# A three-block transformer kernel: an earlier start, a split normalisation, reordered routing, a re-cut fill, and matmuls of constants in five waits

## The reference, cut to what matters

```python
# block 1: differential attention;  block 2: pooling mixer;  block 3: forgetting attention + RG-LRU
h = layer_norm(ALPHA * h + mixer(h), g, b)          # blocks 1 and 2 (block 3: rmsnorm, residual x + mixer)
logits = h @ w_router + b_router                    # 4 group logits, 32 expert logits
g = argmax(group logits); e1, e2 = top2(expert logits of group g)
y[token] = sum_k gate_k * (silu(h @ w_gate[e_k]) * (h @ w_up[e_k])) @ w_down[e_k]
h = layer_norm(ALPHA * h + y, g, b)
# differential attention, per head of 8:
o = (softmax(q1 k1') - lam * softmax(q2 k2')) @ v
o = o * rsqrt(mean(o*o) + 1e-5) * sub_g * (1 - lambda_init)   # then @ w_o
# block 3's attention, per head of 8: softmax(q k' / 8 + decay) @ v, a width of 64
```

## Time and profile before

| | |
|---|---|
| median of 3 runs | 2135.12 us (2132.74 to 2141.25) |
| the profiled execution's own time | 2146.18 us |
| its span, first to last instruction | 2144.1 us |
| mean granted TensorE clock | 0.973 |
| busy: PE, DVE, ACT, POOL | 2006.3, 694.8, 404.4, 117.2 us |

### The profile page before, as it was taken

How to read it: one execution, slowest core, us unless ns; L and a number is a source line. 1 busy time by engine, 2 the same in 40 slices (tenths; PEclk the granted TensorE clock), 3 DMA queues, 4 the chain that set the end, 5 groups by cost and what they waited for, 6 DMA issues and landing times.

```text
span 2144.1 us, 25582 instructions
## 1 busy us (share of the span) xinstructions
PE 2006.3 (94%) x10125; PEld 1074.9 (50%) x10125; DVE 694.8 (32%) x1668; ACT 404.4 (19%) x873; POOL 117.2 (5%) x140
## 2 busy tenths in 40 slices
PE   8999989999999999799999999999699989899787
PEld 4444445545545454645655455454544445665454
DVE  0155546321111111635421111111747223532114
ACT  1033432111111111111111111111233222112112
POOL 0000001100000000000100000000100001111100
PEclk9999998999999999999999999999899999999999
DMA  9611102799999999922799999999921111699995
GB/s 331 176 59 40 40 20 101 275 419 420 420 421 420 421 420 391 334 99 70 285 419 419 421 421 421 421 420 400 330 85 39 39 40 43 208 355 420 419 419 211
DMA packets 123826, 595.59 MB, mean 278 GB/s; under 512 B 15751, under 2 KB 43287, under 8 KB 60767
## 3 DMA queue, kind: packets, MB, share of 16 engines
q1 hardware_dynamic: 110559, 568.06, 66.7%
q0 software_dynamic: 13184, 26.40, 3.7%
HBM read 572.95 MB, written 37.01 MB: 284 GB/s over the span
## 4 chain that ended last, share of the span: by engine, by line
PE 79%; DMA 12%; DVE 5%; ACT 2%; issue 2%; another core or an unknown queue 0%; SPq 0%; DVEq 0%; ACTq 0%
PE bank L979 21%; PE bank L1022 10%; PE bank L653 10%; PE bank L895 10%; DMA ring<-in_moe_w_up_dram 6%; DMA ring<-in_w_up_dram 5%; PE bank L795 5%; PE bank L665 4%; PE bank L639 3%; PE bank L1153 1%; PE bank L749 1%; PE bank L722 1%; PE bank L886 1%; PE bank L1114 1%; PE bank L709 1%
## 5 line engine op out<-in xcount | busy, mean ns | idle before, releaser
L979 PE MATMUL bank<-ring,work 128*64 128x512 f32 (+1 forms) x3008 | 559.5, 523 | 29.2 <-DMA ring<-in_w_up_dram 25.9
L979 PEld LDWEIGHTS bank<-ring,work 128*64 128x64 f32 x3008 | 222.9, 137 | 361.9 <-issue 336.2
L1022 PE MATMUL bank<-ring,work 128*64 128x512 f32 x1280 | 295.8, 600 | 3.9 <-DVE work L1839 3.9
L1839 DVE COPY work<-bank 128x256 f32<-128x256 f32 (+1 forms) x96 | 36.5, 380 | 691.7 <-PE bank L887 691.7
L895 PE MATMUL bank<-work 128*128 128x128 f32 x2112 | 253.3, 278 | 0.0
L895 PEld LDWEIGHTS bank<-work 128*128 128x128 f32 x2112 | 240.8, 192 | 6.3 <-issue 2.0
L653 PE MATMUL bank<-hT,ring 128*128 128x512 f32 x512 | 237.7, 607 | 0.7 <-ACT work L1216 0.7
L1307 ACT ACTIVATE work<-bank 64x512 f32<-64x512 f32 x96 | 56.6, 589 | 547.2 <-PE bank L1022 541.9
L1022 PEld LDWEIGHTS bank<-ring,work 128*64 128x64 f32 x1280 | 84.3, 136 | 143.9 <-issue 129.0
L653 PEld LDWEIGHTS bank<-hT,ring 128*128 128x128 f32 x512 | 94.2, 194 | 109.7 <-issue 107.9
L1295 ACT ACTIVATE work<-bank 64x512 f32<-64x512 f32 (+1 forms) x96 | 49.7, 518 | 475.1 <-PE bank L979 475.1
(11 more groups left out here) (306 smaller groups left out, 1691.8 us busy)
## 6 DMA issues: line engine op xcount, KB each, us to landing
ring<-in_moe_w_down_dram SPq DMA_DIRECT2D x128, 1024.0 KB, 16.7
ring<-in_moe_w_gate_dram SPq DMA_DIRECT2D x126, 1024.0 KB, 15.5
ring<-in_moe_w_up_dram SPq DMA_DIRECT2D x126, 1024.0 KB, 17.3
ring<-in_w_down_dram SPq DMA_DIRECT2D x32, 1024.0 KB, 25.4
ring<-in_w_gate_dram SPq DMA_DIRECT2D x31, 1024.0 KB, 22.9
ring<-in_w_up_dram SPq DMA_DIRECT2D x31, 1024.0 KB, 23.6
ring<-in_attn_w_qkv_dram SPq DMA_DIRECT2D x12, 1024.0 KB, 13.6
work<-y_rows SPq DMA_DIRECT2D x12, 1024.0 KB, 6.9
```

The lines of the kernel that those rows point to most:

```text
L979: mm = pe.matmul(GU2[s % 2][BLK * a:BLK * a + BLK, 0:F], xgT[pair % 2][:, per * kk + k, BLK * of_pair:BLK * of_pair + BLK], v[a][:, k, :], ...
L1022: mm = pe.matmul(DN[BLK * n:BLK * n + BLK, :], hT_[:, 2 * kk + k, :], v[:, k, 512 * n:512 * n + 512], start=(kk + k == 0), stop=(2 * kk + ...
```

## The change

- Start: SP issues unit 0 after the second tile of `x`, units 1 and 2 after the fourth, and the rope table after them. PE turns two tiles, then runs the first unit's matmuls tile by tile (`turn_beside`), turning tiles 2 and 3 between them. POOL's broadcasts wait for the last tile of `x`.
- First attention's end: root and scaling for tiles 0 and 1 are moved ahead (DVE step 39, ACT step 40, before its last `copy_turned`); those for tiles 2 and 3 stay behind the last step. PE turns tiles 0 and 1, begins `head(0)`, and turns tile 2 after `project(0, 0)` and tile 3 after `project(0, 1)`.
- Heads, all three: PE's second half of `project(3, 1)` is moved before `ranks(1)`. DVE's `choose(1)` and `place(0)` are moved before `part(3, 0)`, `place(1)` stays after it; the three memsets go from tile 0 to tile 1.
- `keep_busy(n)` is new: n matmuls of constants, 512 columns each, into bank 0, whose result nobody reads. n = 13 after `sum_last_pair` at the end of mixtures 0 and 1, behind a wait for the gathered rows of tile 0; n = 4 in each head between `gather(2)` and `ranks(3)`.
- `fill`: the same 16 matmuls a head pair are cut otherwise over the steps, and the empty eighth step is dropped, so that pair 2 begins at g = 7 and pair 3 at g = 15.

```diff
             for i in range(T):
                 sp.dma_start(h[:, i, :], t["x"][0, P * i:P * i + P, :]).then_inc(x_loaded[i], 16)
+                if i == 1:
+                    load(0)
+            load(1)
+            load(2)
             sp.dma_start(work[:, 16384:17408], t["rope"]).then_inc(par.rope, 16)
-            for u in range(first["wo"]):
+            for u in range(3, first["wo"]):
                 load(u)
...
+            def keep_busy(n):
+                for _ in range(n):
+                    pe.matmul(bank[0][:, :], ident, con[:, 0:512], start=True, stop=True)
...
                 sum_last_pair(l, 0)
                 sum_last_pair(l, 1)
+                pe.wait_ge(routing.gathered[0], 16 * (l + 1))
+                keep_busy(13)
                 for tt in range(T):
...
                     for tt in range(T):
+                        if ready and kk == 0:
+                            ready(tt)
                         for k in range(4):
...
-            turn("x", h)
-            pe.wait_ge(tiles_copied, turns["x"].copied_all)
-            for n in range(2):
-                project_b(first["v"] + 2 * n, hT, bank[4 * n:4 * n + 4])
+            def turn_beside(tt):
+                if 1 <= tt < T - 1:
+                    turn("x", h, K, range(tt + 1, tt + 2))
+                pe.wait_ge(tiles_copied, 2 * tt + 2)
+
+            turn("x", h, K, range(2))
+            project_b(first["v"], hT, bank[0:4], turn_beside)
+            project_b(first["v"] + 2, hT, bank[4:8])
...
-            turn("o1", o1[:, :, 4 * P:8 * P], 4)
+            def turn_o1(tt):
+                turn("o1", o1[:, :, 4 * P:8 * P], 4, range(tt, tt + 1))
+
+            turn_o1(0)
+            turn_o1(1)
...
                 project(0, 0)
+                if l == 0:
+                    turn_o1(2)
                 project(0, 1)
+                if l == 0:
+                    turn_o1(3)
                 project(1, 0)
...
                 turn_one(2)
+                project(3, 1, range(4, K))
                 ranks(1)
-                project(3, 1, range(4, K))
                 router(2)
...
                 gather(2)
+                keep_busy(4)
                 ranks(3)
...
             for c in range(1, 4):
-                for x, sizes in enumerate((((1, 2), (1, 2), (1, 1)), ((1, 2), (1, 2), (1, 0), (1, 0)))):
+                queries = ((1, 2), (1, 2), (1, 1)) if c == 1 else ((0, 2), (1, 1), (1, 1), (1, 1))
+                for x, sizes in enumerate((queries, ((1, 1), (1, 2), (1, 1), (1, 0)))):
...
-                fill.append([])
...
             for step in range(5 * 8 + 1):
+                if step == 40:
+                    act.wait_ge(at.var, 2)
+                    act.activation(orstd[:, 0:2, 4:8], orstd[:, 0:2, 4:8], ACT.Sqrt).then_inc(at.std, 1)
                 if step > 8:
                     copy_turned(step - 9)
...
+                if step == 39:
+                    dve.wait_ge(at.o, 30)
+                    dve.tensor_scalar(orstd[:, 0:2, 4:8], sumsq[:, 0:2, 4:8], 1.0 / P, 1e-5, ALU.mult, ALU.add)\
+                        .then_inc(at.var, 1)
...
+            for t0 in (0, 2):
+                if t0:
+                    dve.wait_ge(at.o, 32)
...
+                dve.wait_ge(at.std, 2 + t0 // 2)
+                link(dve.reciprocal(orstd[:, t0:t0 + 2, 4:8], orstd[:, t0:t0 + 2, 4:8]))
+                for tt in range(t0, t0 + 2):
+                    for hh in range(4, 8):
+                        ins = normal_head(tt, hh)
+                    ins.then_inc(tiles_written, 1)
...
                 for tt in range(T):
+                    if tt == T - 1:
+                        choose(1)
+                        place(0)
                     part(tt, 0)
...
                     if tt == T - 1:
-                        choose(1)
-                        place(0)
                         place(1)
                     part(tt, 1)
...
+            pool.wait_ge(x_loaded[T - 1], 16)
             bcast(subg, t["attn_sub_g"], par.sublam, 128)
```

More of the change, by code:

```diff
@@ L656, in project_t, with project_b @@
                         mm.then_inc(units_used if half else half_unit, 1)
-            def project_b(u, operand, banks):
+            def project_b(u, operand, banks, ready=None):
                 for kk in range(2):
@@ L1260, in _ @@
                         .then_inc(at.raw, 1)
-            act.wait_ge(at.var, 2)
-            act.activation(orstd[:, :, 4:8], orstd[:, :, 4:8], ACT.Sqrt).then_inc(at.std, 1)
+            act.wait_ge(at.var, 3)
+            act.activation(orstd[:, 2:4, 4:8], orstd[:, 2:4, 4:8], ACT.Sqrt).then_inc(at.std, 1)
             turned("o1", 4)
@@ L1583, in _ @@
             dve.wait_ge(at.added, 8)
[L1584 to L1591, removed]
+            for t0 in (0, 2):
+                if t0:
+                    dve.wait_ge(at.o, 32)
+                    dve.tensor_scalar(orstd[:, 2:4, 4:8], sumsq[:, 2:4, 4:8], 1.0 / P, 1e-5, ALU.mult, ALU.add)\
+                        .then_inc(at.var, 1)
+                dve.wait_ge(at.std, 2 + t0 // 2)
[4 more added lines that the diff above has]
+                    ins.then_inc(tiles_written, 1)
             link(dve.tensor_scalar(slots1, con[:, C_SLOT:C_SLOT + BLK], 1.0, None, ALU.add))
@@ L1689, in mixture @@
                 for tt in range(T):
+                    if tt == T - 1:
+                        choose(1)
+                        place(0)
                     part(tt, 0)
-                    if tt == 0:
+                    if tt == 1:
                         dve.memset(gpad, -BIG)
```

## The result

The changed kernel took 2120.09 us (2118.37 to 2122.30, four runs) against 2135.18 (2132.74 to 2141.25, four runs): a ratio of 0.9919, interval 0.9896 to 0.9942. It is 15 us faster; 31.5 were forecast, and the time lies at the upper edge of the whole range given (2092 to 2120), outside the 2095 to 2112 in which the forecast itself was put. The profiled execution after took 2122.30, with a span of 2120.5: between the two profiled spans 23.6 us are gone, between the medians 15. Both differences need explaining.

What follows compares the result with a forecast made beforehand. PE was taken as the bound (busy 2006 of 2144.1 us), with its idle time and lower-clock work to be won. Eight terms summed to -31.5 us, from 2135.1 to 2103.6; forecast range 2095 to 2112, whole range 2092 to 2120.

Steps and rivals of the forecast that it cites:

- Start, -5.5: Kernel start: values begin 6.9 us earlier, added tile blocks cost 2.1, clock returns 0.7; -5.5 us, between -3 and -7.
- First attention's end, -4.0: End of first attention: `project(0, 0)` 6.0 us earlier, less turned tiles and lower clock; -4.0, between -2.3 and -6.
- head(0), -8.0: Before mixture 0: filled waits, earlier `choose` and constants remove a lower-clock stretch; -8.0 us, between -5 and -11.3.
- head(1), +0.5: Before mixture 1: constants delay `ranks(3)` by 2.4 us, partly given back by quicker gathers; +0.5, between -1.5 and +3.
- head(2), -3.4: Before mixture 2: earlier `ranks(2)`, quicker `gather(3)` and less waiting, against constants costing 2.2; -3.4 us, between 0 and -5.
- Mixture 0's end, 0.0: After mixture 0: 13 constants delay the first turn by 2.5 us; turn and projection give it back; 0.0, -1.8 to +2.5.
- Mixture 1's end, -1.3: After mixture 1: constants fit the wait; turn and projection give 0.9 + 1.5, DVE takes back 1.1; -1.3, 0 to -2.
- Second attention, -9.8: Re-cut fill: 3.7 us less waiting, and lower-clock losses in pairs 1 and 2 won; -9.8, between -3.7 and -10.5.
- rival of constants at the lower clock: Blocks of 13 and heads' fours: constants don't hold the clock, each costs 1.72 us; total 2145 us, chance 0.04.
- Theory 1: Set before follow-ups: terms right in kind; the profiled execution before had a low stretch in head(0) that other executions lack.
- Theory 2: Set before follow-ups, for the missing gain: the matmuls of constants cost what the orders win.
- Theory 3: Set before follow-ups, for the missing gain: what is won early is lost in the weight stream.

Runs made afterwards that it cites:

- end_only: The kernel before with the new end of the first attention alone (and the heads' three memsets behind tile 1): 2130.27 us, ratio 0.9983.
- b_again: The kernel before, unchanged, run and profiled a second time: 2135.36 us, ratio 0.9995 to the kernel before.
- fill_only: The kernel before with the re-cut fill of the second attention alone: 2124.66 us, ratio 0.9940.
- best: The changed kernel without the blocks of 13 constants and with the four constants in head(0) alone: 2106.34 us, ratio 0.9867 to the kernel before.
- after: The changed kernel with all its edits, in its first measurement and profile: 2120.09 us, ratio 0.9919 to the kernel before.
- start_only: The kernel before with the new start alone (SP's order, PE's `turn_beside`, POOL's wait): 2138.36 us, ratio 0.9998.
- no_constants: The changed kernel without any matmuls of constants (both blocks of 13, all three of four): 2114.26 us, ratio 0.9904 to the kernel before.
- a_again: The changed kernel, unchanged, run and profiled a second time: 2116.24 us, ratio 0.9906 to the kernel before.

## Where the prediction was right and where its sum went too far, point by point

- **Start, -5.5.** The values come 6.5 us earlier. The first q and k projection comes at 73.2 to 76.2, mean 74.6, in the five traces with the old start and at 67.5 to 71.2, mean 69.2, in the nine with the new one: -5.4. Right for the place. By itself it moved no median; six of its twelve runs lie where head(0)'s bad outcome was traced.
- **First attention's end, -4.0.** It is 5.2 to 6.1 shorter, less the 1.05 of turned tiles that went into head(0): 4.1 to 5.0, and 4.1 by `end_only`. Load and root took 1.49 and left 0.96 of the cover, as the rows said and not as the Trainium skill has it (ScalarE: Activation LUTs, What ACT_TABLE_LOAD costs), whose 1.38 of drain would have used it up: no drain is to be seen between the load's end at 306.45 and the root at 306.47.
- **head(0), -8.0: the step that failed**, together with the sentence "A difference carries over". Profile to profile it measured -9.2. Against the ordinary execution, `b_again`, it is +0.5 to -0.1: 59.0 before, 59.5 and 58.9 after, with the 1.05 of turned tiles counted above in it, so that the term itself is -0.5 to -1.2. It is made of the order, about +1 (60.1 and 60.3 without tiles and constants), and the four constants, about -2 (61.0 and 61.1 without, 58.6 to 59.5 with them). The prediction had noted that the profiled execution lay 11 us above the median, and didn't ask which of its terms was made of those 11. The low stretch at 0.50 and the wait of 4.55, whose cause it had not found in the trace, were just that. A part of the low clock it named did stay: the first gather still takes 3.78.
- **head(1), +0.5.** It measured +2.3 between the profiles, +2.2 to 2.9 against `b_again`, inside the bound of 3. How much of it the fours are isn't settled: without them it took 83.5 to 87.0 in five traces with the new order, with them 85.3 to 86.6 in four.
- **head(2), -3.4.** It measured -3.0. The parts were other than forecast in size: the order gives 6 (60 to 54.0) where only 1.0 to 1.2 of issue wait stands before the last gather, and the fours take back 2.8.
- **Mixture 0's end, 0.0.** It measured +1.8 and -1.6, as worked out; against `b_again` +1.8 and -0.9.
- **Mixture 1's end, -1.3, the other step that failed.** It measured +3.7: 2.4 up to the sums, most of it the wait on issue, 1.7 for the sums at the lower clock, and the turn gave 0.65 for 0.9. The first projection gave nothing: after 3.52 us idle it was at the lower clock as before. The prediction had no term for a wait that 21 more matmuls ahead bring with them.
- **Second attention, -9.8.** It measured -8.6 between the profiles, -9.9 to -12.4 against `b_again`; -11 to -13 by `fill_only`. Eight steps took 29.6 where 29.5 was forecast for a pair, but only in the middle; the first eight took 33.0.
- **A part that no edit touches:** the eight matmuls of eight rows took 11.58 after and 8.65 in `best`, as the clock fell in them early or late. That is 2.8 of the profiled pair's difference; the interval is 12.3 to 12.6 in four traces, with the change's parts and without them (`after`, `fill_only`, `start_only`, `end_only`), and 9.4 to 10.2 in the other ten.
- **Sums in it that are off.** The good ends of the terms add up to 45.1, so 2090 and not 2092. In the rival of constants at the lower clock the fours delay `ranks(3)` by 5.7 only in heads 1 and 2; against head(0)'s wait of 3.93 it is 3.0, so 14.5 in all and not 17. Neither changes the forecast.

From -31.5 to the -23.6 of the profiled pair: mixture 1's end 5.0, the eight-row matmuls 2.8, head(1) 1.8, and the others -1.7 together. From -23.6 to the -15 of the medians: before's profiled execution lay 11.0 above its median, after's 2.2. On the second chip the medians differ by 19.7. Counted against an ordinary execution, head(0) misses some 7, mixture 1's end 5.0 and head(1) 1.8; with these the forecast would have been about -18, between the two differences measured. That the time still fell into the range given owes something to the range: its upper end was there for other cases, some edits that miss and clock stretches that only move.

Theory 1 holds for the larger part. Theory 2 holds for the fours in head(2) (2.8) and for mixture 1's end (over 3), about 6 us in all; the gains in head(0) (2) and in the projections after mixture 0 (1.5, against a delay of 1.8) give back about 2 of it. That `no_constants` is no faster for all that has to do with its waits on issue, 1.34 in head(0) and 2.48 in head(2), where `best` has none and 0.97. `best`, without the 13s and those fours, lies 0.4% (8 us) under `a_again` by the ratios. Theory 3 falls: mixtures 0 and 1 take 470 to 475 us and mixture 2 278, however early they start. The rival of constants at the lower clock falls with 0.86 us each.

## What to carry to other kernels

Before a term of a sum is read from a profile, set that execution's own time against the median: if it lies above by more than most runs scatter, some stretch in it may be bad luck, and a second profiled execution of the same kernel says which. Here an order that takes waits away (the fill, 11 us) was worth far more than filler that occupies them. The filler paid 2 us in head(0), where work at the lower clock stood behind it, about nothing after mixture 0, and cost 2.8 in head(2), where only 0.96 was idle. A wait longer than the filler was no guarantee either: after mixture 1, 3.52 us stayed idle behind it and the projection was at the lower clock as before. A gain that doesn't show in the median may be there in half the executions; look at the single times before calling it nothing.

## What the runs showed of the hardware that was not expected

- The same idle time of 2.36 us before `ranks(1)` was followed by 17 us at the lower level (1.2 GHz, a granted 0.50 and 0.51) in two traces; in three others the same 17 us had 0.90, 0.90 and 0.80, the rest being at 2.4 GHz (`b_again`, `fill_only`, `end_only`). What decides isn't visible here. Both long executions also have DVE's wait of 4.55 before its last logits, and in `b_again` and `fill_only` it is 0.60 and 0.61.
- The clock also fell where PE had no wait at all: in the eight matmuls of eight rows PE was busy throughout, and the granted clock went from 0.92 to 0.50, in `after` for their last 8.6 us, in `best` for their last 2.7.
- A wait of PE on issue came and went with what stands ahead in its program: 3.2 to 3.4 before mixture 1's last sums in all three kernels with 21 more matmuls ahead, none on issue there in the other eleven traces. Before the last gathers of head(1) and head(2) no such rule shows: the profile puts waits of 0.97 to 2.67 on issue in some traces and of 0.74 to 3.65 on DVE in others, in head(1) even for one and the same program (2.08 on DVE in before, 1.41 on issue in `b_again`). The instructions come in packets of about 16 KB (0.92 MB in 56, the page's q8 row). That these waits are for such packets was not shown.
- Matmuls of the identity by constants keep the clock up like any other: 11.32 us for 13.
